# The opening of a streaming-encoder block: four weight lists instead of three, and the first rows normalised in pairs

## What is computed

```python
h = layer_norm(x, in_ln_g, in_ln_b)
proj = h @ w_in                                  # 1024 -> 1792
q, k, v, u = split(proj)                         # 512, 128, 128, 1024
attn = swa_gqa_with_sinks(rotary(q), rotary(k), v, sinks)   # windows of 128 keys
a, gate = split(u)                               # 512, 512
conv = silu(layer_norm(causal_depthwise_conv31(a * sigmoid(gate))))
h = layer_norm(ALPHA * h + concat(attn, conv) @ w_o)
h = layer_norm(ALPHA * h + conv_gated_mlp(h))
```

## Time and profile before

| | us |
|---|---|
| median of 3 runs | 1901.73 (1900.45 to 1901.87) |
| span of the profiled execution | 1897.6 |
| TensorE busy | 1859.7 (98%) |
| VectorE busy | 1515.5 (80%) |
| ScalarE busy | 959.7 (51%) |
| GpSimd busy | 894.1 (47%) |
| mean granted TensorE clock | 0.997 of full |

### The profile page before, as it was taken

How to read it: one execution, slowest core, us unless ns; L and a number is a source line. 1 busy time by engine, 2 the same in 40 slices (tenths; PEclk the granted TensorE clock), 3 DMA queues, 4 the chain that set the end, 5 groups by cost and what they waited for, 6 DMA issues and landing times.

```text
span 1897.6 us, 27021 instructions
## 1 busy us (share of the span) xinstructions
PE 1859.7 (98%) x8632; PEld 1526.1 (80%) x8632; DVE 1515.5 (80%) x1926; ACT 959.7 (51%) x1503; POOL 894.1 (47%) x666
## 2 busy tenths in 40 slices
PE   8999999999999799999999999999999999999998
PEld 7788888777777688888888778888888788888886
DVE  8777994799998887888888988878787755776787
ACT  4555662777778544444445544444444432232453
POOL 2169994266675354345445544444442875430000
PEclk9999999999999999999999999999999999999999
DMA  7411123644563423333334333232324644587554
GB/s 279 175 44 44 44 83 123 207 132 142 172 207 116 144 106 130 130 116 105 122 138 172 118 116 111 99 111 94 106 104 157 189 153 142 163 265 246 183 170 145
DMA packets 201829, 265.80 MB, mean 140 GB/s; under 512 B 12320, under 2 KB 131360, under 8 KB 200480
## 3 DMA queue, kind: packets, MB, share of 16 engines
q1 hardware_dynamic: 188096, 229.32, 36.7%
q10 hardware_dynamic: 13664, 35.66, 5.1%
HBM read 177.18 MB, written 87.75 MB: 140 GB/s over the span
## 4 chain that ended last, share of the span: by engine, by line
PE 72%; DVE 11%; issue 5%; ACT 4%; DMA 4%; POOL 3%; SPq 1%; DVEq 0%; POOLq 0%; ACTq 0%
PE u_mm L2408 35%; PE d_y L2837 21%; PE a_mm L254 14%; DMA u_w_raw<-w_up 2%; ACT m_ce L1781 1%; PE m_y L2457 1%; ACT m_tps L1773 1%; DVE m_stat L2192 1%; DVE m_top L2236 1%; DVE m_den L2249 1%; DVE u_forms L1962 1%; DVE u_w_lo L1953 1%; PE a_acc L658 1%; DMA d_wd_raw<-w_down 1%; ACT m_probT L1828 1%
## 5 line engine op out<-in xcount | busy, mean ns | idle before, releaser
L2408 PE MATMUL u_mm<-u_forms,u_w_hi 128*128 128x512 f32 x2464 | 761.1, 390 | 8.7 <-DVE u_forms L1962 3.4
L2408 PEld LDWEIGHTS u_mm<-u_forms,u_w_hi 128*128 128x128 f32 x2464 | 462.2, 188 | 108.8 <-issue 11.0
L2408 PE MATMUL u_mm<-u_forms,u_w_lo 128*128 128x512 f32 x1232 | 479.9, 390 | 0.0
L2837 PE MATMUL d_y<-d_wd,d_a_hi 128*128 128x512 f32 x1232 | 379.4, 389 | 2.6 <-DVE d_a_lo L1054 2.0
L254 PE MATMUL a_mm<-a_hT,a_w_hi 128*128 128x512 f32 x896 | 278.1, 392 | 1.5 <-DVE a_hT L557 1.5
L2837 PEld LDWEIGHTS d_y<-d_wd,d_a_hi 128*128 128x128 f32 x1232 | 231.1, 188 | 51.3 <-DVE d_a_lo L1054 2.4
L2408 PEld LDWEIGHTS u_mm<-u_forms,u_w_lo 128*128 128x128 f32 x1232 | 231.5, 188 | 48.2
L2837 PE MATMUL d_y<-d_wd,d_a_lo 128*128 128x512 f32 x616 | 239.6, 389 | 0.0
L1993 DVE SCALAR_TENSOR_TENSOR u_y<-u_z,u_taps,u_y 128x1024 f32<-128x1024 f32 x176 | 222.6, 1287 | 10.4 <-DVE u_z L2007 3.2
L254 PEld LDWEIGHTS a_mm<-a_hT,a_w_hi 128*128 128x128 f32 x896 | 166.7, 188 | 37.0 <-DVE a_hT L557 3.0
L1363 POOL TENSOR_TENSOR u_w_sum<-u_w_raw 128x512 f32<-128x512 f32 x44 | 59.4, 1349 | 263.9 <-DMA u_w_raw<-w_up 258.2
(11 more groups left out here) (250 smaller groups left out, 2944.8 us busy)
## 6 DMA issues: line engine op xcount, KB each, us to landing
u_w_raw<-w_up SPq DMA_DIRECT2D x44, 1024.0 KB, 5.2
d_a_raw<-gated_scr SPq DMA_DIRECT2D x56, 704.0 KB, 5.3
gated_scr<-u_s SPq DMA_DIRECT2D x88, 256.0 KB, 2.0
d_wd_raw<-w_down SPq DMA_DIRECT2D x88, 256.0 KB, 5.2
gated_scr<-u_gy SPq DMA_DIRECT2D x44, 256.0 KB, 2.2
a_xs<-x SPq DMA_DIRECT2D x16, 512.0 KB, 5.7
m_h_in<-h_scr SPq DMA_DIRECT2D x16, 512.0 KB, 3.9
h_scr<-m_r SPq DMA_DIRECT2D x16, 512.0 KB, 4.7
```

The lines of the kernel that those rows point to most:

```text
L2408: last = nc.tensor.matmul(mm[BANK[s]][:], w[:, s, k, :], forms[:, POS[s], part, k, :], start=(s in FRESH and k == 0 and w is w_hi and part ...
L2837: m = nc.tensor.matmul(dy[u % BANKS][:], a[:, u % 2, k, :], wd[:, ph % 2, k, part, :], start=(k == 0 and a is a_hi and part == HI_PART), s ...
```

## The change

The number of lists in the opening goes from three to four (a 0, gate 0, qkv 0, qkv 1), so block n is multiplied in 32 steps instead of 24 while block n + 1 is normalised, and nine lists follow before the values instead of ten. The fourth list gets tiles of its own for its split weights. The rows of block 0 are normalised in two pairs: statistics, root, scale and shift of rows 0 and 1, then those of rows 2 and 3, all scale and shift on VectorE; ScalarE takes the moments of row 2 there. Loads of x, of the norm's rows and of the lists are put in another order, the identity is loaded from ScalarE's queue, and `AHEAD`, the counts of `keep_busy` and ScalarE's order are written anew. The partial sums of all four convolutions come one list later, those of j = 3 behind lists 10 and 11; so do the stores but for the last, which stays behind list 11.

```diff
-STREAM = [("a", 0), ("gate", 0), ("qkv", 0)] + [(_kind, _j) for _j in range(1, CT) for _kind in ("a", "gate")]
-STREAM += [("qkv", _j) for _j in range(1, QT)]
-OPEN = 3
+STREAM = [("a", 0), ("gate", 0), ("qkv", 0), ("qkv", 1)] + [(_kind, _j) for _j in range(1, CT) for _kind in ("a", "gate")]
+STREAM += [("qkv", _j) for _j in range(2, QT)]
+OPEN = 4
...
+        w4_hi, w4_lo = sb("a_w4_hi", [P, KT, P], F32R), sb("a_w4_lo", [P, KT, P], F32R)
...
-        CONV_DONE = [("a", 2), ("a", 3), ("qkv", 1), ("qkv", 3)]
+        CONV_DONE = [("a", 2), ("a", 3), ("qkv", 2), ("qkv", 3)]
...
-        BY_ACT, BY_DVE = 1, (0, 2, 3)
+        ACT_ROW = (2, 1, 1, 1)
...
@@ the sync queue @@
+            first_row(0)
+            first_row(1)
+            sp.dma_start(g_bc, row_to_all(ln_g)).then_inc(g_ld, 16)
+            sp.dma_start(b_bc, row_to_all(ln_b)).then_inc(b_ld, 16)
+            load_list(0)
+            first_row(2)
+            first_row(3)
+            load_list(1)
+            load_list(2)
+            reload(0, 0)
+            reload(0, 1)
+            store(0, 0)
+            store(0, 1)
+            sp.wait_ge(wlo_ok, 1)
+            load_list(3)
...
@@ ScalarE @@
+            def take_early_q(n, j):
+
+                e = OPEN * n + 2 + j
+                act.wait_ge(mm_ok, e + 1)
+                act.wait_ge(q_st[j], 16 * (n + 1))
+                nc.scalar.copy(q_out[:, j, :], mm[2 + j][:]).then_inc(mm_free, 1)
+                act.wait_ge(mm_free, e + 1)
+                act.dma_start(qkv_scr[j, :, bass.ts(n, BLK)], q_out[:, j, :]).then_inc(q_st[j], 16)
+
+            act.dma_start(ident[:], con[:, CON_ID:CON_ID + P]).then_inc(con_ld, 16)
...
+            take_root(1, 0, 2)
             hi_of(0, 0)
             weights_hi(0)
             hi_of(0, 1)
             weights_hi(1)
+            moments(0)
+            take_root(2, 2, RB)
+            weights_hi(2)
+            weights_hi(3)
             hi_of(0, 2)
             hi_of(0, 3)
             moments(1)
+            take_root(3, 0, RB)
+            nc.scalar.preload_act_table(ACT.Sigmoid)
+            norm_last(1)
+            take_a(0, 0, 0, 0)
+            take_gate(1, 0, 1)
+            hi_of(1, 0)
+            take_early_q(0, 0)
+            hi_of(1, 1)
+            moments(2)
+            hi_of(1, 2)
+            take_early_q(0, 1)
+            hi_of(1, 3)
+            take_root(4, 0, RB)
+            take_a(OPEN, 0, 1, 0)
+            norm_last(2)
+            take_gate(OPEN + 1, 1, 1)
+            hi_of(2, 0)
+            hi_of(2, 1)
+            hi_of(2, 2)
+            take_early_q(1, 0)
+            hi_of(2, 3)
+            moments(3)
+            take_early_q(1, 1)
+            take_root(5, 0, RB)
+            norm_last(3)
+            take_a(2 * OPEN, 0, 2, 0)
+            hi_of(3, 0)
...
-                    if 1 <= j < 3:
-                        tap_products(CT - 1, NB * (j - 1) + n)
+                    if j < 4:
+                        tap_products(CT - 1, NB * (j - 2) + n)
...
@@ VectorE, block 0 @@
+            for r in range(HALF_ROWS):
+                dve.wait_ge(x_ld[r], 16)
+                half_stats(0, r, 0)
+                half_stats(0, r, 1)
+            chain.wait()
+            for r in range(HALF_ROWS):
+                aggregate(r)
+            chain.wait()
+            roots(1, 0, HALF_ROWS)
             dve.wait_ge(g_ld, 16)
-            rows(0)
+            for r in range(HALF_ROWS):
+                scale(0, r)
+                shift(0, r)
+            lo_of(0, 0)
+            dve.wait_ge(x_ld[3], 16)
+            half_stats(0, 3, 0)
+            lo_of(0, 1)
+            half_stats(0, 3, 1)
+            chain.wait()
+            aggregate(3)
+            chain.wait()
+            dve.wait_ge(moment_ok, 3)
+            roots(2, HALF_ROWS, RB)
+            assert chain.n == OPENING
+            for r in range(HALF_ROWS, RB):
+                scale(0, r)
+                shift(0, r)
             stats(1, 0)
             lo_of(0, 2)
+            stats(1, 2)
             lo_of(0, 3)
-            stats(1, 2)
...
@@ TensorE @@
-            AHEAD = {1: (14, 17, 19, 21), 2: (12, 15, 18, 21), 3: (12, 15, 18, 21)}
+            AHEAD = {1: (14, 20, 25, 29), 2: (16, 20, 23, 27), 3: (8, 13, 16, 21)}
...
-            with pe.Fori(0, 9) as _:
+            with pe.Fori(0, 8) as _:
                 keep_busy(8)
-            for r, count in enumerate((8, 16, 0, 16)):
-                transposes(0, r)
-                keep_busy(count)
+            transposes(0, 0)
+            keep_busy(16)
+            transposes(0, 1)
+            keep_busy(16)
+            transposes(0, 2)
+            transposes(0, 3)
...
+            lists(OPEN, 1)
+            with pe.Fori(0, (LAST - OPEN - 1) // 2) as q:
+                lists(2 * q + (OPEN + 1), 0)
+                lists(2 * q + (OPEN + 2), 1)
...
-    nc = bacc.Bacc("TRN2", target_bir_lowering=False, num_devices=1)
+    nc = bacc.Bacc("TRN2", target_bir_lowering=False, num_devices=1, dynamic_dma_scratch_size=512)
```

More of the change, by code:

```diff
@@ L260, in _, with first_row @@
         def _(sp):
[L261 to L265, removed]
             def load_list(i):
                 sp.dma_start(list_raw(i), w_tiles[i, :, :, :]).then_inc(list_landed(i)[0], 16)
+            def first_row(r):
+                sp.dma_start(xs[:, r, :], x[bass.ts(r, P), :]).then_inc(x_ld[r], 16)
             def reload(n, r):
@@ L277, in store @@
                 sp.dma_start(h_scr[RB * n + r, :, :], row(n, r)).then_inc(h_st[r], 16)
-            for i in range(OPEN):
-                load_list(i)
+            first_row(0)
[13 more added lines that the diff above has]
+            load_list(3)
             sp.dma_start(taps[:], par[:, PAR_TAPS:PAR_TAPS + CT * TAPS].rearrange("p (c t) -> p c t", c=CT)).then_inc(pos_ld, 16)
             sp.dma_start(cbias[:], par[:, PAR_CB:PAR_CB + CT]).then_inc(pos_ld, 16)
-            for n in range(NB - 1):
+            reload(0, 2)
+            reload(0, 3)
+            store(0, 2)
+            store(0, 3)
+            for n in range(1, NB - 1):
                 reload(n, 0)
@@ L288, in _ @@
                 store(n, RB - 1)
-            for i in range(OPEN, OPEN + 2):
-                sp.wait_ge(wlo_ok, i - OPEN + 1)
-                load_list(i)
+            sp.wait_ge(wlo_ok, 2)
+            load_list(4)
+            sp.wait_ge(wlo_ok, 4)
+            load_list(5)
             for r in range(RB):
                 store(NB - 1, r)
-            for i in range(OPEN + 2, len(STREAM)):
+            for i in range(6, len(STREAM)):
                 sp.wait_ge(wlo_ok, i - 1)
@@ L508, in _, with block_base, half_stats, aggregate @@
             chain = Count(dve_seq, dve)
[L510 removed]
+            HALF_ROWS = 2
+            OPENING = 2 * 3 + 3 + 2 * 4
+            STEPS = 2 * 3 + 3 + 4
+            def block_base(n):
+                return OPENING + STEPS * (n - 1)
+            def half_stats(n, r, a):
+                chain.inc(nc.vector.bn_stats(stat[:, r, a, :], xs[:, r, a * BLK:(a + 1) * BLK]))
             def stats(n, r):
[L513 removed]
+                chain.base, chain.n = block_base(n), 2 * dve_rows(n).index(r)
                 dve.wait_ge(x_ld[r], n * 16 + 16)
                 for a in range(2):
[L516 removed]
+                    half_stats(n, r, a)
+            def aggregate(r):
+                chain.inc(nc.vector.bn_aggr(mv[:, r, :], stat[:, r, :, :].rearrange("p a s -> p (a s)")))
+            def roots(count, first, last):
+                at = slice(first, last)
+                nc.vector.tensor_scalar(veps[:, at], mv[:, at, 1], EPS, None, ALU.add).then_inc(veps_ok, 1)
+                dve.wait_ge(root_ok, count)
+                chain.inc(nc.vector.reciprocal(inv[:, at], root[:, at]))
+                dve.wait_ge(veps_ok, count)
+                refine_rstd(nc, chain, rstd[:, at], veps[:, at], inv[:, at], tmp[:, at])
+                chain.wait()
             def block_stats(n):
                 chain.wait()
[L520 to L521 removed]
+                for r in dve_rows(n):
+                    aggregate(r)
                 chain.wait()
                 dve.wait_ge(moment_ok, 3 * n + 3)
[L524 to L529 removed]
+                roots(n + 2, 0, RB)
                 nc.vector.scalar_tensor_tensor(out=nmr[:], in0=mv[:, :, 0], scalar=-1.0, in1=rstd, op0=ALU.mult,
```

117 lines of the change are left out of this document (46 added, 71 removed).

## The result

The changed kernel takes **1935.09 us** (median of 4, 1932.61 to 1936.31) against 1901.32 us for the kernel before on the same chip: ratio **1.0179, interval 1.0164 to 1.0193**, 33.8 us slower. Forecast were 24.0 us more, at most 29. The sign was right, the size and the range were not. The profiled execution took 1932.61 us, its span is 1930.8, so 33.2 us longer than the one before.

What follows compares the result with a forecast made beforehand. The prediction took TensorE, busy 98% of the span, as the bound, its work unchanged. Opening 10.4, idle before attention 12.4, less 0.8, clock 2.0 gave 24.0 us more: 1901.73 + 24.0 = 1925.7 us; own range 1918 to 1931, stated range 1912 to 1931.

Steps and rivals of the forecast that it cites:

- First sweep: Opening, block 0: TensorE's first sweep starts at 31.3, 4.25 us later, with VectorE doing all eight scale and shift passes.
- Clock at the start: First sweeps in the opening: they start at half clock after TensorE stood still, losing 2.0 us, bounds 0 and 2.2.
- Gap (a): Between blocks 0 and 1: TensorE idle 3.5 us, as ScalarE's take of the fourth list stands ahead of row 3's high part.
- Gap (b): Between blocks 2 and 3: TensorE waits 2.0 us for block 3's row 0 behind ScalarE's take, store and root table load.
- rival 4: Clock also falls in the gap between blocks 0 and 1, and gaps are a little longer: 1929.5 us; chance 0.09.
- The opening's shift: Opening in all: 4.25 + 2.0 + 3.5 + 2.0 - 1.35 = 10.4 us later at equal numbers of sweeps, bounds 5 and 14.
- The convolutions: VectorE's convolutions start one list (21.8 us) later; the last ends at 317.8 on the old clock of lists.
- Idle ahead of the means: Start of attention: means can start at 336.4 on the old clock, leaving TensorE idle 12.4 us; whole part's bounds 9 and 16.
- From the means to pv: Attention's start: half clock costs 2.0 us, and 0.8 comes back from the wait for ScalarE behind the output weights.
- Rivals 1: Only attention's start is late, the opening neutral as VectorE's pairs overlap better: 12.3 us more, 1914.0; chance 0.12.
- 2: Only the opening is late, the convolutions find 12 us of slack: 10.4 us more, 1912.1; chance 0.08.
- 3: Not slower: the first convolution's 11.54 us wait for GpSimd shrinks to nothing: 1901.4 us; chance 0.05.

Runs made afterwards that it cites:

- e2: Changed kernel with GpSimd held until block 0's four rows are shifted before making low parts of lists 2 and 3: first sweep 3.6 us earlier, first pv product 3.3 earlier.
- e7: Changed kernel with 68 more filler transposes ahead of row 2, 20 before row 3, 18 behind: first sweep to block 1's 29.17 us instead of 31.70.
- e4: Changed kernel with the last 8 of the first stage's 31 convolution taps left out on VectorE, ScalarE and GpSimd: 7.3 us less by the medians.
- e6: Changed kernel with only block 0's rows, loads and fillers taken back to the old way, four lists kept: 12.1 of the 33.8 us gone.
- e3: Changed kernel with block 1's row 3 high part ahead of the take of block 0's fourth list on ScalarE: medians 3.7 us less.
- e8: Changed kernel with identity first in SP's queue, GpSimd held, block 1's row 3 first, more fillers, list 13 of blocks 0 and 1 before the means: 1921.65 us.
- e10: Changed kernel with block 0's old rows, block 1's row 3 first, list 13 of blocks 0 and 1 ahead of the second stage's waits: 1914.57 us.
- e11: Changed kernel with e8's five repairs, list 13 of blocks 0 and 1 now ahead of the second stage's waits: 1915.00 us.

## Why the prediction was wrong in size

**First sweep: predicted 31.3, measured 37.08. This is the step that failed**, the sentence "Roots 1.3, two rows 2.5 each: row 2 ready at 24.0, row 3 at 26.6". It priced VectorE's passes by rows where GpSimd was idle and didn't ask what GpSimd does in those microseconds, though the same working has ScalarE's copy of list 3's weights end at 25, and GpSimd's remainders of lists 2 and 3 follow ScalarE's copies. Those cost 4.05 us (3.24 + 3.37 - 2 x 1.28, and e2's 23.47 - 19.42). The sign was in the trace of before, unread; from the timelines of VectorE and of GpSimd:

```profile
29.79 1.94 DVE L524 TENSOR_SCALAR a_vs<-a_mv 128x4 f32<-128x4 f32 x1
```

```profile
29.31 2.39 POOL L455 TENSOR_TENSOR a_w_lo<-a_q_out,a_w_hi 128x1024 fp32r<-128x1024 f32 x1 [1.08 <-ACT a_w_hi L302]
```

An operation on four columns, 0.17 us elsewhere, took 1.94 and ended at 31.73, when GpSimd's instruction did (31.70). The Trainium skill (SBUF — State Buffer, Who interferes with whom) states the rule: a VectorE instruction with two inputs in SBUF contends with a GpSimd one that reads SBUF for a shared port pair, which one of them holds for its whole instruction while the other waits. This case's passes agree: one that waits out GpSimd's 2.35 us and then takes its own 1.28 would need at most 3.6 (an estimate from these two durations), and they took 3.24 and 3.37. Passes over whole rows with only one input tile in SBUF keep their length beside GpSimd: the low part at 18.34 (1.22 us, its other input is in PSUM) beside the subtraction of 16.72 to 19.10, and the row statistics at 19.49 (0.68) beside that of 19.34 to 21.69. So do the convolution's passes, the same operation on 128x1024 with the sum `a_acc` in PSUM. From the trace of before, VectorE and GpSimd:

```profile
126.42 1.28 DVE L637 SCALAR_TENSOR_TENSOR a_acc<-a_gb,a_ctaps,a_acc 128x1024 f32<-128x1024 f32 x1
124.13 4.64 POOL L492 TENSOR_TENSOR a_gb<-a_gb,a_spare 128x513 f32<-128x513 f32 x4 [0.77 <-ACT a_spare L411]
```

The 1.94 us operation has a single input, `a_mv`, so what is said above of two inputs doesn't cover it; that it waited is seen, why it did wasn't tested.

The other 1.7 us: the identity. The prediction had row 0 ready at 11.75, and it was, at 11.63; but TensorE was still in its 64 fillers until 13.6, since the identity's load, moved to ScalarE's queue, let it start at 4.92 instead of 2.80. Row 2's moments, behind it, end at 21.82 instead of 20.15. I moved the issue in my sum and not what hangs on its landing.

**Clock at the start: predicted 2.0, measured 2.5** (14 steps in 12.20 us instead of 9.66; e7 gives the same 2.5). Right in its mechanism; over the executions it was 1.5 to 2.8, so the bound of 2.2 was too low. That transposes alone hold the clock, which the prediction took from 1.00 over 72 of them, is shown by e7.

**Gap (a): 3.5, measured 3.37. Gap (b): 2.0, measured 1.83.** Right, each in its place and with its releaser. (The 3.3 that the prediction gives for (b) with a drain should be 2.0 + 1.38 = 3.4; the load of the root's table at 97.17, 1.28 us, was followed by the root at 98.47, so no drain is seen.) But (a) also brought the clock down, 1.6 us, which stood only in the bounds and in rival 4. With the earlier trace rows at hand, where 3.41 us of idleness had done it, that belonged into the forecast.

**The opening's shift.** 10.0 + 2.5 + 3.4 + 1.6 + 1.8 - 1.35 = 18.0; list 12 and the convolutions are 17.3 later; 0.7 is left over.

**The convolutions.** Predicted: one list (21.8) later than before plus the opening's shift. 295.98 + 21.8 + 17.3 = 335.1; measured 335.08. The mechanism holds to a tenth, the first convolution's wait for GpSimd is 11.54 us as before, and e4 shows the link behind it.

**Idle ahead of the means: 12.4, measured 13.86.** Predicted were 4.4 us from the store's issue to the constants' load and 14.15 from there to the last sum's end. Measured are 5.36 (335.11 to 340.47) and 14.61 (to 355.08). The first excess has its cause in the queue: eight loads for the rotation stand ahead of the constants. Before, they were through long before the store landed; now they are issued directly behind the last convolution, take 2.94 + 1.67 us and end at 340.37, while GpSimd saw the store landed by 339.17. I counted the landing and not what the queue still had to issue. This is read from the trace; no run tests it. The second excess, 0.5, stays open.

**From the means to pv: predicted 2.0 - 0.8 = 1.2, measured 19.77 - 17.94 = 1.8.** The clock cost 2.2; of the 0.8 only 0.3 came back: TensorE waits 0.58 instead of 0.91 for ScalarE.

In all, of 33.1 - 24.0 = 9.1 us that were missing in the trace, 5.8 are the first sweep, 1.6 the clock in gap (a), 1.5 the idle ahead of the means, 0.6 the stretch behind it, 0.5 the clock at the start: 10.0, less 0.3 of the two gaps and the 0.7 left over, so that 0.1 stays open. Rivals 1 and 2 are refuted by e6 (both parts are late), and 3 by the 11.54 us that didn't shrink. Of rival 4 the clock in gap (a) was there, 1.6 us; its longer gaps were not.

## What to carry to other kernels

Before a pass is moved to VectorE, look at what GpSimd does in the same microseconds: here a VectorE pass with both inputs in SBUF and a GpSimd subtraction didn't run side by side, and the price was a whole instruction of the other engine, so keep them apart, cut the one off the critical path small, or have one input in PSUM, as the convolution has (read from its passes; not tried on the rows). When one more unit of work goes ahead of a long side chain (here convolutions), its whole length, less the cover that the chain had, becomes idle time of the main engine unless the order gives that engine something else, ahead of every wait that belongs to the chain; here that won back about half. A load that is moved to another queue is judged by who waits for its landing. And before two profiles are subtracted, see that the stretch ahead of the edit ran alike in both: here the fillers and the half clock behind them differed by 1.3 and 1.4 us from one execution to the next, as much as some of the edits were worth.

## What the runs showed that I had not expected

- A VectorE operation on 128x4 elements took 1.94 us instead of 0.17, and four GpSimd quarters 6.76 us instead of 2.79, where they met instructions of the other engine.
- Behind 1.9 us of idle TensorE the granted clock was 0.50 in e3 (69 to 72 us), e8 (60 to 63 us) and e10 (59 to 62), and behind the same 1.9 us it stayed at 1.00 in e11 (64 to 72 us).
- Fillers of 128x128 f32 transposes held the clock at 1.00 for 19.5 us in e7 with gaps of 1.4 to 1.6 us between them. But the first 64 of an execution run at 6 to 7 per us at first and at 10 to 11 later, with the granted clock at 1.00 throughout; where the change comes (at 8 us in the changed kernel, after 11 in e7) makes their 8.85 to 10.12 us. Why is open.
- The same opening differs between executions: row 0's transposes start at 12.67 in e8 and, with the rows of x landing later (7.63), at 14.64 in e11. The first sweeps of two such executions, 32.10 and 35.79, differ by more than most of the edits here.
